# A two-layer hybrid decoder step on one core: decode tokens taken out of the prompt's products, and cache loads dealt out anew

## The reference, cut to what matters

```python
def rmsnorm(x, g): return x * rsqrt(mean(x * x, -1) + 1e-6) * g

# layer 0: h = rmsnorm(x, g0); split(h @ w_in) -> da_q, da_k, da_v, g_q, g_k, g_v, g_lr, g_og
# differential attention, 4 heads; q, k hold two halves of 64, v has 128 columns
a = softmax(q1 @ k1.T * scale + bias) - lam * softmax(q2 @ k2.T * scale + bias)
a_out = rmsnorm(a @ v, g_da) * (1 - lam_init)       # samples: 32 pages of 128 cached k and v, and the new token
# gated linear attention, 4 heads, in chunks of 16 tokens, state S of 64 x 128
S = exp(b_last) * S + kd.T @ v                      # serial over the prompt's 32 chunks
o = rmsnorm(o, g_gla) * silu(g_og)
x = x + rmsnorm(concat(a_out, o) @ w_out, g1)
x = x + rmsnorm(square(relu(rmsnorm(x, g2) @ w_up)) @ w_down, g3)     # w_up 1024 x 4096

# layer 1: Griffin block (two projections of 1024, causal convolution, gates, linear scan, w_out), then an MLP as above
```

## Time and profile before

| | |
|---|---|
| runs | 1537.25, 1544.59, 1545.81 us; median 1544.59 |
| span of the profiled execution, first to last instruction | 1541.8 us (its device time stands in no other figure) |
| PE busy | 1406.3 us, 91% |
| DVE, ACT, POOL busy | 882.3, 516.7, 328.7 us |
| mean granted TensorE clock | 0.930 of 2.4 GHz |
| moved by DMA | 249.32 MB, of it 134.23 MB on GpSimd's queue (the cache) and 107.13 MB on SyncE's |

### The profile page before, as it was taken

The page is one execution under the profiler, slowest core; times in us unless marked ns, Lnnn a source line. Parts: engine busy times, 40 slices in busy tenths (PEclk is TensorE's granted clock), DMA queues, the critical chain, the costliest instruction groups (busy, mean ns, idle before and its releaser), DMA issues.

```text
span 1541.8 us, 26106 instructions
## 1 busy us (share of the span) xinstructions
PE 1406.3 (91%) x11324; PEld 1266.3 (82%) x11324; DVE 882.3 (57%) x1156; ACT 516.7 (34%) x839; POOL 328.7 (21%) x264
## 2 busy tenths in 40 slices
PE   4999957788778698999999999899989999999997
PEld 3999933345334398999999999899989999999997
DVE  3398978766988526624435343689556344353443
ACT  3323254433423424312212122469443122131233
POOL 1085768865777100000000000000000000000000
PEclk8999979877676799999999999999999999999999
DMA  9477699988989831232322322222212323223211
GB/s 320 137 264 232 236 327 382 369 324 326 346 322 346 300 109 55 86 106 83 97 97 82 99 94 83 83 83 83 85 55 88 105 83 101 92 83 103 90 55 56
DMA packets 126856, 249.32 MB, mean 162 GB/s; under 512 B 5251, under 2 KB 107415, under 8 KB 110096
## 3 DMA queue, kind: packets, MB, share of 16 engines
q0 software_dynamic: 18432, 134.23, 22.9%
q1 hardware_dynamic: 103616, 107.13, 21.5%
q10 hardware_dynamic: 4696, 6.32, 1.3%
HBM read 239.99 MB, written 7.73 MB: 161 GB/s over the span
## 4 chain that ended last, share of the span: by engine, by line
PE 58%; issue 25%; DVE 7%; POOL 4%; DMA 3%; ACT 3%; ACTq 0%; POOLq 0%; DVEq 0%
PE PS L1881 46%; PE PS L2074 2%; POOL PROD L680 2%; DMA KV<-in_cache_v,CIDX 2%; DVE SC L1352 1%; PE PS L2216 1%; POOL KV L747 1%; DVE ST L1584 1%; PE PS L2061 1%; PE PS L2158 1%; DMA XSIN<-in_x_sample 1%; PE PS L1865 1%; PE PS L2179 1%; PE PS L2116 1%; PE PS L1975 1%
## 5 line engine op out<-in xcount | busy, mean ns | idle before, releaser
L1881 PE MATMUL PS<-H_hi,W_hi 128*128 128x260 f32 x1936 | 397.7, 287 | 16.7 <-DVE H_lo L1327 9.7
L1881 PE MATMUL PS<-H_hi,W_lo 128*128 128x260 f32 x1936 | 393.4, 285 | 0.0
L1881 PE MATMUL PS<-H_lo,W_hi 128*128 128x260 f32 x1936 | 393.0, 285 | 0.0
L1881 PEld LDWEIGHTS PS<-H_hi,W_hi 128*128 128x128 f32 x1936 | 303.2, 191 | 22.3 <-issue 17.7
L1881 PEld LDWEIGHTS PS<-H_hi,W_lo 128*128 128x128 f32 x1936 | 301.9, 191 | 0.0
L1881 PEld LDWEIGHTS PS<-H_lo,W_hi 128*128 128x128 f32 x1936 | 301.7, 191 | 0.0
L1285 DVE TENSOR_TENSOR W_lo<-RAW,W_hi 128x2048 fp32r<-128x2048 f32 x90 | 208.2, 2313 | 125.9 <-ACT W_hi L810 125.8
L810 ACT ACTIVATE W_hi<-RAW 128x2048 fp32r<-128x2048 f32 x90 | 171.8, 1909 | 266.1 <-PE PS L1881 265.5
L1881 PE MATMUL PS<-U_hi,W_lo 128*128 128x260 f32 x1024 | 206.4, 283 | 0.0
L1881 PE MATMUL PS<-U_lo,W_hi 128*128 128x260 f32 x1024 | 206.0, 283 | 0.0
L1881 PE MATMUL PS<-U_hi,W_hi 128*128 128x260 f32 x1024 | 206.0, 282 | 0.0
(11 more groups left out here) (304 smaller groups left out, 1433.8 us busy)
## 6 DMA issues: line engine op xcount, KB each, us to landing
RAW<-in_w_up SPq DMA_DIRECT2D x32, 1024.0 KB
RAW<-in_w_down SPq DMA_DIRECT2D x32, 1024.0 KB
RAW<-in_w_in_even SPq DMA_DIRECT2D x13, 1024.0 KB
RAW<-in_w_in_odd SPq DMA_DIRECT2D x8, 1024.0 KB
RAW<-in_w_out_even SPq DMA_DIRECT2D x4, 1024.0 KB
RAW<-in_w_out_odd SPq DMA_DIRECT2D x4, 1024.0 KB
x_saved<-X ACTq DMA_DIRECT2D x1, 2080.0 KB, 9.3
X<-x_saved SPq DMA_DIRECT2D x1, 2080.0 KB, 7.8
```

What stands on the lines that cost most here:

```text
L1881: t = MM_(PS[:, 2 * bank + j, 0:HALF], w[:, ch.slot, k, cols], x[:, k, half], start=k == 0 and n == 0, stop=k == KT - 1 and n == 2)
```

## The change

The eight decode tokens leave the dense products of the output projection and of layer 0's MLP. There the prompt alone is multiplied, 512 columns in one bank, one matmul where there were two. The decode tokens follow as work of their own between the tiles (`sample(t)` on TensorE, VectorE and ScalarE, for tile t of the MLP): GpSimd loads the same weights again in float32, 36 chunks of 1 MB (4 of w_out, 16 of w_up, 16 of w_down), into three buffers of the ring; the weights stream as the moving operand (256 columns) past a stationary operand of 32 columns (the 8 tokens repeated four times), 8 products a chunk, one for each input tile, in the four column groups; ScalarE copies the partial sums out (`part`), and TensorE adds up the groups and transposes by 8 float32 products (`folds`) six times. The samples' attention output is finished between tiles 3 and 8 of the MLP instead of before the output projection.

The last 16 v-chunks are no longer read in the GLA units: 4 are read right behind them, 12 between the tiles of the output projection. Each attention unit takes 2 k-chunks instead of 1; the GLA units take 1, 0, 1, 0, 1, 0, 1, 0 k-chunks and 2 v-chunks each. From load 114 on only the four buffers off X are used. One table of v-weights (PM) moves for the second half. Some semaphores are merged (`exp_asked`, `exp_given`), and the last unit's power is computed earlier on GpSimd.

```diff
-    UNIT_STEPS = [1] * 16
-    GLA_STEPS = [3, 3, 3, 3, 3, 3, 2, 0]
+    UNIT_STEPS = [2] * 16
+    GLA_STEPS = [1, 0] * 4
...
-            take("kvkvkv" if n == 3 else "kvkvv" if n == 2 else "vvv")
+            take("k" * n + "vv")
         take("v" * (64 - v))
-        return order
+        return order + [("w", n) for n in range(36)]
+    ALL_SIX, SAMPLE_RING = 114, 3
+    def buffer(i):
+        return i % RING if i < ALL_SIX else (i - ALL_SIX) % 4 if i < LOADS else (i - LOADS) % SAMPLE_RING
+    SAMPLE_MLP, SAMPLE_PERIOD = 21, 8
@@ gpsimd
+            if (kind, n) == ("w", SAMPLE_RING):
+                zero_acc(0)
+            if BEFORE[i] is not None:
+                while used <= BEFORE[i]:
+                    use(used)
+                    used += 1
+            if kind == "w":
+                po.dma_start(weights_of(n), sample_weights(n)).then_inc(kv_loaded[BUFFER[i]], 16)
@@ scalar
-        act.wait_ge(mm_ready, 1)
-        A(E1[:], E1[:], ACT.Exp)
-        A(E2[:], E2[:], ACT.Exp).then_inc(mm_exp, 1)
         split_hi(Chunk(C_OUT0))
-        past_output(1)
...
+        def part(n, banks_):
+            act.wait_ge(w_used, 4 if n == 0 else 36 if n == 9 else 8 * ((n - 1) // 2) + 6 + 2 * ((n - 1) % 2))
+            if n >= 1:
+                act.wait_ge(fold_done, (n + 1) // 2)
+            for i, bank in banks_:
+                t = A(SE[:, 512 * i:512 * i + 512], PS[:, bank, :], ACT.Copy)
+            t.then_inc(part_copied, 1)
@@ tensor: step
             for n, (w, x) in enumerate(((W_hi, hi), (W_hi, lo), (W_lo, hi))):
+                if prompt_only(ch):
+                    t = MM_(PS[:, bank, :], w[:, ch.slot, k, cols], x[:, k, 0:SEQ], start=k == 0 and n == 0, stop=k == KT - 1 and n == 2)
+                    continue
                 for j, half in enumerate(halves):
@@ tensor
+        def sample_products(n, op, bank, fresh):
+            i = place("w", n)
+            pe.wait_ge(kv_loaded[BUFFER[i]], LANDED[i])
+            for r in range(2):
+                for c in range(4):
+                    k = 4 * r + c
+                    t = MM_(PS[32 * c:32 * c + 32, bank, 256 * (n % 2):256 * (n % 2) + 256], op[:, k], weights_of(n)[:, k],
+                            start=fresh and r == 0, stop=r == 1, skip_group_check=True)
+            t.then_inc(w_used, 1)
+        def folds(n):
+            pe.wait_ge(part_copied, min(2 * n + 1, 10))
+            for k in range(KT):
+                t = MM_(PS[:, 6, 64 + 8 * k:72 + 8 * k], SE[:, P * k:P * k + P], FOLD[:, 0:8], start=True, stop=True)
+            t.then_inc(fold_done, 1)
+        def sample(t):
+            if t == 4: ...          # the sums and past_output(1) that stood before the output projection
+            if t in (10, 11):       # w_out, two chunks after each of these tiles
+            g, at = group_step(t)   # at = (t - 21) % 8 in group g = (t - 21) // 8
+            if at in (0, 1):        # w_up of group g, two chunks after each of these tiles
+            if at == 3:
+                folds(g + 1)
+            if at in (5, 6):        # w_down of group g, two chunks after each of these tiles
@@ tensor: end of the GLA units (a third v-chunk of each unit is removed above)
+        v_chunks(48, 4)
         pe.wait_ge(st_ready, 64)
+        normalise(23)
+        def values_behind(t):
+            slot(OUT_SLOT + t)
+            if t < 6:
+                v_chunks(52 + 2 * t, 2)
+        stage(C_OUT0, 4, 1, values_behind)
-        pe.wait_ge(new_ready, 1)
-        stage(C_OUT0, 4, 1)
```

More of the change, by code:

```diff
@@ L523, in trunk, with weights_of, group_step @@
     LOADS = 128
+    ALL_SIX, SAMPLE_RING = 114, 3
+    def buffer(i):
+        return i % RING if i < ALL_SIX else (i - ALL_SIX) % 4 if i < LOADS else (i - LOADS) % SAMPLE_RING
+    BUFFER = [buffer(i) for i in range(len(ORDER))]
+    BEFORE = [max([j for j in range(i) if BUFFER[j] == BUFFER[i]], default=None) for i in range(len(ORDER))]
+    LANDED = [16 * BUFFER[:i + 1].count(BUFFER[i]) for i in range(len(ORDER))]
+    def weights_of(n):
+        return KV[BUFFER[place("w", n)]].rearrange("p n f -> p (n f)").rearrange("p (k n) -> p k n", k=KT)
+    SAMPLE_CHUNKS = [((what, g), j) for g in range(4) for what in ("up", "down") for j in range(4)]
+    SAMPLE_MLP, SAMPLE_PERIOD = 21, 8
+    SAMPLE_END = SAMPLE_MLP + 3 * SAMPLE_PERIOD + 6
+    def group_step(t):
+        g, at = divmod(t - SAMPLE_MLP, SAMPLE_PERIOD)
+        return (g, at) if 0 <= g < 4 and t >= SAMPLE_MLP else (None, None)
     UNITS = [(h, qb) for h in range(HEADS) for qb in range(4)]
@@ L711, in release @@
             kind, n = ORDER[i]
[L712 to L718 removed]
+            freed(po, i)
+            if kind == "v" and n < 32 and n in POWER_BEHIND_V:
+                power(POWER_BEHIND_V[n])
         def weights_behind(i):
@@ L1132, in mlp, with fold_rooted @@
                         before_odd()
-                    if j < 4:
-                        for i in range(2):
-                            u = 2 * j + i
+                    for i in range(2):
+                        u = 2 * j + i
+                        if j < 4:
                             raised(Chunk(c), i, u, 32 * layer + 8 * g + u)
+                        if layer == 0:
+                            sample(16 * g + u)
+        def fold_rooted(n):
+            act.wait_ge(new_held, n + 2)
+            A(MP[:, 8:16], MP[:, 0:8], ACT.Sqrt, scale=1.0 / D_MODEL, bias=EPSC[:, 0:1]).then_inc(new_root, 1)
@@ L1915, in set_ready, with stage @@
             return lambda k: pe.wait_ge(h_ready, 8 * m + k + 1)
-        def stage(c0, count, m):
+        def stage(c0, count, m, after=lambda t: None):
             for j in range(count):
-                products(Chunk(c0 + j), H_hi, H_lo, set_ready(m) if j == 0 else None)
+                products(Chunk(c0 + j), H_hi, H_lo, set_ready(m) if j == 0 else None, lambda i: after(2 * j + i))
         def opening(opened, c0, m):
@@ L1946, in mlp @@
             for g in range(4):
+                after = lambda j: (lambda i: sample(16 * g + 2 * j + i)) if layer == 0 else None
                 for j in range(2 if g == 0 else 0, 4):
-                    products(Chunk(c0 + j, g), H_hi, H_lo)
+                    products(Chunk(c0 + j, g), H_hi, H_lo, None, after(j))
                 for j in range(4, 8):
                     products(Chunk(c0 + j, g), U_hi, U_lo,
-                             (lambda k, g=g: pe.wait_ge(u_lo_ready, g * 8 + (32 * layer + k + 1))) if j == 4 else None)
+                             (lambda k, g=g: pe.wait_ge(u_lo_ready, g * 8 + (32 * layer + k + 1))) if j == 4 else None, after(j))
@@ new lines, in fold_sum, with sample @@
+        def fold_sum(n):
+            pe.wait_ge(new_sq, n + 2)
+            MM_(PS[:, 7, 64 * n:64 * n + 64], ONES[:], E1[:], start=True, stop=True).then_inc(new_summed, 1)
+        def sample(t):
+            if t == 4:
+                pe.wait_ge(ssum_ready, 8)
+                pe.wait_ge(snm_ready, 8)
+                MM_(PS[:, 5, 256:320], ONES[0:8], MDIAG[:].rearrange("j b i -> j (b i)"), start=True, stop=True)
+                MM_(PS[:, 5, 320:384], ONES[:], ROWSUM[:].rearrange("p b j -> p (b j)"), start=True, stop=True).then_inc(smz_done, 1)
+                past_output(1)
+            if t == 7:
+                pe.wait_ge(rs_copied, 1)
+                pe.wait_ge(new_sq, 1)
+                MM_(PS[:, 6, 0:KT * N_SAMPLE], ONES[:], MM[:], start=True, stop=True).then_inc(new_summed, 1)
+            if t in (10, 11):
+                pe.wait_ge(operand_ready, 1)
+                for n in range(2):
+                    sample_products(2 * (t - 10) + n, XM, 3 if t == 10 else 5, True)
+            if t == 13:
+                folds(0)
+            if t == 15:
+                fold_sum(0)
+            if t == 18:
+                fold_sum(1)
+            g, at = group_step(t)
+            if at in (0, 1):
+                pe.wait_ge(operand_ready, 2)
+                for n in range(2):
+                    sample_products(4 + 8 * g + 2 * at + n, XH, 2 + 2 * at, True)
+            if at == 3:
+                folds(g + 1)
+            if at in (5, 6):
+                pe.wait_ge(operand_ready, g + 3)
+                for n in range(2):
+                    sample_products(4 + 8 * g + 4 + 2 * (at - 5) + n, XU[:, g % 2], 3 if at == 5 else 5, g == 0 and n == 0)
+            if t == SAMPLE_END + 2:
+                folds(5)
+            if t == SAMPLE_END + 4:
+                fold_sum(2)
```

394 lines of the change are left out of this document (253 added, 141 removed).

## The result

| | before | after |
|---|---|---|
| median of 4 runs | 1542.7 us (1537.3 to 1545.8) | 1615.8 us (1611.9 to 1621.6) |
| ratio, 95% interval | | 1.0478 (1.0444 to 1.0512): slower |
| span of the profiled execution | 1541.8 us | 1619.7 us |
| mean granted clock of TensorE | 0.930 | 0.917 |

What follows compares the result with a forecast made beforehand. TensorE was taken to bound the MLP, cache loads, closely followed by DVE and POOL, the attention and GLA units. 53.6 - 42.1 - 10 + 6.7 + 11.8 + 5 = +25.0 us gave 1569.6 us, range 1541 to 1599.

Steps and rivals of the forecast that it cites:

- From this nearest row I take 216 ns.: Output projection and layer 0's MLP: a 512-column product takes 216 ns, from float32 records of 432 ns; removes 36.6 us in the MLP.
- The rival that scaled it, 236 ns: Output projection and MLP: the 260-column pace scales to 512 columns, MLP term +42, 1600 us; chance 0.05.
- GLA units: Eight GLA units: 17 us for the first, 12.6 us for each of seven, 105.2 us in all, -42.1 us.
- The seam: Last unit to the projection's first product, 27 us before: sample work leaves, W_hi and W_lo still follow H; -10 us.
- Attention units: 15 attention-unit steps: four loads at 3.16 us make 12.6 us a unit instead of 9.03; +53.6 us.
- the two terms of the deal: Key and value chunks dealt anew: attention units +53.6 us, GLA units -42.1 us.
- Output projection: 192 products of 512 columns plus twelve v-chunks and six switches: 54.4 us instead of 47.72, +6.7 us.
- Decode work in the MLP: Layer 0's MLP: weight chunks, folds, sums and switches add 48.4 us on TensorE; waits for the second weight copy +5 us.
- The third rival's case: Second weight copy late: issue and landing take 9 us, nine places wait 2 to 3 us; about 1590 us, chance 0.15.
- the lead computed for it, 6.9 us: MLP: the fourth chunk of two neighbouring steps can only be requested 6.9 us before TensorE wants it.

Runs made afterwards that it cites:

- e10: The kernel before with one column of the moving operand repeated 260 times in the products of its projections and MLPs (results not computed); 1485.1 us, ratio 0.9616.
- e4: The changed kernel with one column of the moving operand repeated 512 times in output projection and first MLP (results not the reference's); 1588.1 us, ratio 1.0293.
- e5: The changed kernel with the first value chunk of each GLA unit moved behind its update products; 1615.8 us, ratio 1.0482.
- e2: The changed kernel with SyncE waiting until out_gla_prompt has landed before issuing out_gla_sample and the reload of X; 1613.6 us, ratio 1.0460.
- e1: The changed kernel with key chunks dealt as before: one per attention unit, 3, 3, 3, 3, 3, 3, 2, 0 in the GLA units; 1581.7 us, ratio 1.0246.
- e6: The changed kernel with an even deal: 22 key chunks in the attention units, 2 in each of the first seven GLA units; 1586.0 us, ratio 1.0274.
- e3: The changed kernel without decode rows past the GLA units: 36 weight loads and all steps from the tenth on left out; 1567.7 us, ratio 1.0145.
- e11: As e3, but with the 36 weight loads and TensorE's waits for them kept; 1588.3 us, ratio 1.0279.
- e12: As e11, with each buffer of the second weight copy freed one tile earlier; 1566.6 us, ratio 1.0160.
- e9: The changed kernel with ten read patterns of the moving operand, by chunk, in output projection and first MLP (results not the reference's); ran once, 1724.2 us.

## Why the prediction was wrong

The predicted time, 1569.6 us, missed the median by 46.2 us; the span of the profiled execution missed by 52.9 us (+77.9 against +25.0), and this comes apart as follows.

**The step that failed: "From this nearest row I take 216 ns."** A 512-column product took 232.8 ns (mean of 1623). 1536 x 16.8 = 25.8 us in the MLP and 192 x 16.8 = 3.2 us in the projection, 29 of the 52.9 us; without them the time would have lain inside the stated range. The nearest row was of float32 products, each of them two records of 432 ns over 512 columns. If such a record reads its 2048 bytes in 432 ns, that is 4.7 bytes a ns, too slow for the read to show. The row that resembled it less, 260 columns of the rounded kind at 119.9 ns, bore the same limit as the new product, 8.7 bytes a ns (e10). The rival that scaled it, 236 ns, had the right mechanism, a pace per column, and got 0.05. Its 236 was 1.4% off, my 216 was 7%. 260 columns lie 11.6 ns over 260 / 2.4 GHz; by taking 216, 2.7 ns over 512 / 2.4 GHz, I left it out. Even charged once to each instruction it would have given 225. e4 and e10 show that it belongs to the reading of the columns.

**GLA units, -31.4 instead of -42.1.** I took a unit's serial work as 12.0 us plus 0.6 for half a key chunk; it was 13.97 (97.8 us for seven), and the first 18.1 instead of 17. The third value chunk's 1 us was taken off as if it alone stood there. In the chain of after (under e5) ACT's copy PJ (L1025) now leads from the normalisation to the outputs: from L2359's start to L2443's it is 1.4 us, against 1.6 for the same two products in the earlier trace rows with the chunk between them, so only 0.2 us were gained. e5 shows the same of another chunk: 1.86 us taken out moved nothing. The rest is read from the trace and was not tried: units 2 to 4 took 13.0 to 13.2 us at a mean clock of 0.74 to 0.76, while the unit I had taken as the pattern, 13.0 us, had 0.87, and the other four took 13.7 to 15.8. Units 2 and 4 have a key chunk and are only 0.1 and 0.2 us longer than unit 3 (where I had 1.2); in unit 6, the longest, VectorE was at the last key chunk's work from 509.39 to 514.36 us, and half of the update products waited for the mask behind it, at a clock of 0.61:

```profile
514.90 1.97 PE L2428 MATMUL PS<-GVT,KDM 128*64 128x128 f32 x16 [0.74 <-DVE ATTM L1699]
```

That the transfers rest there was right (0.52).

**The seam, -1.7 instead of -10.** The sample work did go, and the step that W_hi and W_lo have to follow with 4.0 us was right: e2's seam is 16.2 us, near the 17 I named. I listed what leaves the chain and not what is issued beside it: ACT sends out_gla_prompt just ahead, and its first H_hi waits until that has landed (L1114). 128 KB, issued from 538.98 us among 3 MB and three cache loads, let it start at 552.67. The 8.3 us are those of the profiled execution; three other profiles had the short seam without e2's edit, so they are in part chance.

**Attention units, +57.1 instead of +53.6.** Right. 12.84 us a unit for four loads are 3.21 us a load, against the 3.16 I took from the earlier trace rows; those six units had 35 loads and not 36, which gives 3.25 and would have been nearer. e1 gives the unit back its 9.0 us. The prediction had the two terms of the deal at +53.6 and -42.1; e1 and e6 show what makes it a loss: it moves key chunks from where one costs 1.7 us to where one costs 3.3 to 3.8.

**Output projection, +12.4 instead of +6.7.** Besides the 3.2 us of the read: the first tile took 8.65 us instead of 24 x 0.2328 = 5.59 while the clock was low, 1.4 us more than the 1.7 I carried over, and six pairs of value chunks took 1.85 us plus some 0.2 us of restart each, 12.3 us against 11.2.

**Decode work in the MLP.** 48.4 us of work and 5 us of waits, 53.4, against 53.1: 51.5 measured by e3, of which 5.9 were waits, and the sums before tile 10, 1.6 us, which e3 keeps. A pair of products took 1.86 us (0.93 each, 0.86 predicted), a fold 1.68 (1.78). The third rival's case, 9 us to the landing and waits of 2 to 3 us at nine places, did not come in after (6.2 and 8.1 us, 5.9 us of waits in all); it came in e11, where the lead was shorter, and went in e12 with the landing still at 9. So the lead computed for it, 6.9 us, was the right thing to look at. Whether descriptors written by GpSimd make the landing long was not tried.

**The sum** then: 29.0 (read) + 10.7 (GLA) + 8.3 (seam) + 3.5 (units) + 2.5 (first tile and value chunks) - 0.3 (decode) = 53.7 us. The stages of the table missed by 53.3 together, the span by 52.9.

## What to carry to other kernels

Before a product is made wider, ask what the narrow one is bound by: here both are bound by reading the moving operand at about 4 bytes per 0.45 ns, so half as many instructions save 3% of TensorE's time, half of that because 512 columns are 1.5% fewer than 520, and eight more columns of decode in each product (under 10 us in this MLP, by e3) are far cheaper than a second pass over the weights at 50 us. A row of another number format is no nearest row, however equal its shape; divide its time by its bytes as well as by its columns. When a step is taken off a chain, look for its twin on the other engines (something else that is due at the same time), and when a load's lead is shorter than its landing, move the request by one step before blaming the traffic.

## What the runs showed of the hardware

- The read of a float32 moving operand limits TensorE at full clock: 232.8 ns for 512 columns, 216.0 when one column is repeated or each is used twice.
- Every second float32 column costs double (453 ns for 256 columns read twice, 233 for 256 side by side read twice), though a bf16 taken every 4 bytes costs 226.
- With a stationary operand of 128 x 128 for each product, products of 128 columns followed one another at 112 ns in the median, with one column repeated as well, and those of 260 columns with one column repeated at 112.6 in the mean. In one chunk of e9 the products of 128 columns took 208 ns each on average: the granted clock had fallen to half (1.2 GHz) with TensorE busy throughout, some 14 us after the end of a wait of 7.5 us for weights; whether the wait has to do with it is not shown. Windows of e9, that chunk and another of the same pattern:

```profile
1075.00:1096.00 21.00, 21.00 (x100) 21.00 (x100) 1.81 (x3) 0.63 (x1) 0.00 (x0) 0.50 0.00 0
800.00:811.00 11.00, 11.00 (x106) 10.59 (x98) 3.41 (x3) 2.52 (x3) 1.87 (x2) 1.00 0.84 267
```

- A 1 MB load of weights issued by GpSimd, at 1 KB a row, cost its queue 0.9 us, and landed after 6.2 us (up) and 8.1 us (down) in the median in after, 9.0 and 9.3 in e12.
